# Dilated attention over shared keys in 24 rounds of one group and two heads

## What is computed

```python
def dilated_group(q, k, v, slopes, window, dilation):    # one of three (window, dilation)
    ...
    scores = einsum(q, k) / sqrt(64)                     # 16 heads of 64
    bias = -slopes * distance
    scores = where(valid, scores + bias, NEG_INF)        # causal, within the window, on the dilation's grid
    m = max(scores); p = exp(scores - m); denom = sum(p)
    return p / denom @ v, m + log(denom)

def dilated_attention(x, k, v, w_q, w_o):
    q = (x @ w_q).reshape(bsz, s, 3, 16, 64)             # one set of queries for each group
    outs, lses = [dilated_group(q[:, :, g], k, v, ...) for g in range(3)]
    out = sum(softmax(lses) * outs)
    return out.reshape(bsz, s, 1024) @ w_o
```

## Times and profile before

| what | us |
| --- | --- |
| median of 3 runs | 1826.42 |
| lowest and highest | 1825.64, 1828.47 |
| the profiled execution | 1825.73 |
| its span, first to last instruction | 1824.0 |
| TensorE, VectorE, ScalarE busy in the span | 1772.3, 1290.3, 977.8 |

### The profile page before, as it was taken

The page is one execution under the profiler, slowest core; times in us unless marked ns, Lnnn a source line. Parts: engine busy times, 40 slices in busy tenths (PEclk is TensorE's granted clock), DMA queues, the critical chain, the costliest instruction groups (busy, mean ns, idle before and its releaser), DMA issues.

```text
span 1824.0 us, 33247 instructions
## 1 busy us (share of the span) xinstructions
PE 1772.3 (97%) x11768; PEld 1607.0 (88%) x11768; DVE 1290.3 (71%) x2099; ACT 977.8 (54%) x1706; POOL 0.2 (0%) x4
## 2 busy tenths in 40 slices
PE   8999998999999999999899998999999999999998
PEld 7888998888899888888788888878999988798887
DVE  6776789777655776678877766758656576677765
ACT  5563694655355564555565635454534354556553
POOL 0000000000000000000000000000000000000000
PEclk9999999999999999999999999999999999989999
DMA  7665465466545665323446652333556533346662
GB/s 223 188 205 188 123 197 166 152 189 214 172 143 180 185 201 190 116 93 105 173 153 187 208 182 86 111 104 117 162 172 202 168 98 126 98 131 186 190 206 87
DMA packets 76637, 290.77 MB, mean 159 GB/s; under 512 B 9344, under 2 KB 11648, under 8 KB 76544
## 3 DMA queue, kind: packets, MB, share of 16 engines
q1 hardware_dynamic: 76544, 289.50, 50.2%
HBM read 288.42 MB, written 1.05 MB: 159 GB/s over the span
## 4 chain that ended last, share of the span: by engine, by line
PE 88%; DVE 7%; ACT 3%; issue 1%; DMA 0%; SPq 0%; ACTq 0%; DVEq 0%
PE psum L500 32%; PE psum L501 16%; PE psum L492 11%; PE psum L494 10%; PE psum L493 10%; DVE wlo L1505 2%; PE psum L738 1%; PE psum L632 1%; PE psum L627 1%; DVE r L1677 1%; PE psum L579 1%; PE psum L737 1%; ACT whi L1043 1%; PE psum L860 1%; PE psum L867 1%
## 5 line engine op out<-in xcount | busy, mean ns | idle before, releaser
L1505 DVE TENSOR_TENSOR wlo<-raw,whi 128x1024 fp32r<-128x1024 f32 (+3 forms) x496 | 644.8, 1309 | 262.3 <-ACT whi L1043 261.5
L500 PE MATMUL psum<-x_split,whi 128*128 128x512 f32 x1760 | 618.7, 395 | 4.5 <-DVE x_split L1540 3.4
L1043 ACT ACTIVATE whi<-raw 128x1024 fp32r<-128x1024 f32 (+3 forms) x496 | 548.8, 1119 | 43.0 <-PE psum L494 24.4
L501 PE MATMUL psum<-x_split,wlo 128*128 128x256 f32 x1760 | 494.2, 281 | 0.0
L500 PEld LDWEIGHTS psum<-x_split,whi 128*128 128x128 f32 x1760 | 331.3, 188 | 82.9 <-DVE x_split L1540 2.7
L492 PE MATMUL psum<-x_split,whi 128*128 128x272 f32 (+1 forms) x1184 | 349.4, 295 | 9.8 <-DVE wlo L1505 4.9
L494 PE MATMUL psum<-x_split,wlo 128*128 128x272 f32 (+1 forms) x1184 | 341.4, 288 | 0.0
L493 PE MATMUL psum<-x_split,whi 128*128 128x272 f32 (+1 forms) x1184 | 340.6, 288 | 0.0
L501 PEld LDWEIGHTS psum<-x_split,wlo 128*128 128x128 f32 x1760 | 331.7, 188 | 0.0
L500 PE MATMUL psum<-h_split,whi 128*128 128x512 f32 x770 | 272.2, 397 | 0.0
L492 PEld LDWEIGHTS psum<-x_split,whi 128*128 128x128 f32 x1184 | 226.3, 191 | 20.9 <-issue 14.7
(11 more groups left out here) (230 smaller groups left out, 1767.1 us busy)
## 6 DMA issues: line engine op xcount, KB each, us to landing
raw<-w_in SPq DMA_DIRECT2D x264, 512.0 KB, 3.6
raw<-w_out SPq DMA_DIRECT2D x96, 704.0 KB, 4.3
raw<-w_mix SPq DMA_DIRECT2D x44, 512.0 KB, 3.6
raw<-w_rg SPq DMA_DIRECT2D x25, 512.0 KB, 4.1
raw<-w_q SPq DMA_DIRECT2D x24, 512.0 KB, 3.8
raw<-w_mixo SPq DMA_DIRECT2D x16, 576.0 KB, 3.7
raw<-w_kv SPq DMA_DIRECT2D x16, 512.0 KB, 3.6
raw<-w_rg_out SPq DMA_DIRECT2D x8, 640.0 KB, 3.9
```

Source lines behind the costliest of these rows:

```text
L500: nc.tensor.matmul(ps[:, bank, :], whi[slot][:, w], split, start=start, stop=False)
L501: return nc.tensor.matmul(part(bank, 0), wlo[slot][:, w], split[:, 0], start=False, stop=stop)
L1043: nc.scalar.activation(whi[slot][:, 0:cols], raw[slot][:, 0:cols], ACT.Copy).then_inc(w_hi_done, count)
L1505: V.tensor_tensor(wlo[slot][:, 0:cols], raw[slot][:, 0:cols], f(whi[slot][:, 0:cols]), ALU.subtract).then_inc(w_lo_done, 1)
```

## The change

The attention stage runs in rounds, one behind each projection tile. Round n takes pair n // 3 and group n % 3, and both heads of the pair.

- `scores(n)`: four matmuls, the two heads alternating, head e to bank 2 + 2 (n % 2) + e; it waits for its own projection tile and for VectorE's reading of round n - 2 (`round_biased`).
- `bias_max(n)`: four fused instructions (scores plus distance, times minus the slope, and the minimum), for each head and token tile, and at the third group a small minimum over groups. The slope's reciprocal is folded into the scale of the queries (`C_QS`, eight more columns of parameters). `exps` takes the negative.
- `sum_groups(a)`: one addition and two fused instructions (addition and scaling) in place of two additions and two scalings.
- `values(hp)`: both heads of a pair, alternating, in one bank (7); transposes go to bank 6.
- Two buffers of scores for a pair each: `s_even`, and `s_odd` in rows of `h_split` that are free in this stage.
- After the last tile six steps follow, in which the output projection is begun on three tiles: seven products deep on the first two and five on the third.
- The semaphore counts of the hybrid layers no longer include the attention's sixteen heads.

Of the three loops over s in the diff, the first is TensorE's, the second ScalarE's and the third VectorE's.

```diff
-            def scores(a):
-                hp, rows = a // 2, slice(HD * (a % 2), HD * (a % 2 + 1))
-                pe.wait_ge(acc_free, st.u0 + GROUPS * (hp + 1))
-                if a:
-                    pe.wait_ge(biased, a)
-                for g in range(GROUPS):
-                    nc.tensor.matmul(ps[:, 2 + g, 0:P], qT[rows, hp % 2, g, 0:P], kT[rows, hp, 0:P], start=True, stop=True)
-                    last = nc.tensor.matmul(ps[:, 2 + g, P:SCORES], qT[rows, hp % 2, g, P:SEQ], kT[rows, hp, :],
-                                            start=True, stop=True)
-                last.then_inc(scored, 1)
+            def scores(n):
+                hp, g = n // GROUPS, n % GROUPS
+                pe.wait_ge(acc_free, st.u0 + n + 1)
+                if n >= 2:
+                    pe.wait_ge(round_biased, n - 1)
+                for queries, keys in ((slice(0, P), slice(0, P)), (slice(P, SEQ), slice(0, SEQ))):
+                    for e in range(2):
+                        rows = slice(HD * e, HD * (e + 1))
+                        cols = TOKEN_TILES[queries.start // P]
+                        last = nc.tensor.matmul(ps[:, round_bank(n, e), cols], qT[rows, hp % 2, g, queries], kT[rows, hp, keys],
+                                                start=True, stop=True)
+                last.then_inc(round_scored, 1)
...
+            def values(hp):
+                pe.wait_ge(pT_copied, 2 * hp + 2)
+                if hp:
+                    pe.wait_ge(at_ready, hp)
+                for t in range(2):
+                    for e in range(2):
+                        a = 2 * hp + e
+                        ins = nc.tensor.matmul(ps[HD * e:HD * (e + 1), 7, P * t:SEQ], v_tok[:, t, HD * a:HD * (a + 1)],
+                                               pT[:, e, SEQ * t:SEQ * t + SEQ - P * t], start=t == 0, stop=t == 1,
+                                               skip_group_check=True)
+                        if t:
+                            ins.then_inc(pv_done, 1)
...
+            for s in range(Q_TILES + 6):
+                if s < Q_TILES:
+                    query(s)
+                if s == Q_TILES:
+                    begin_output(0, range(0, 3))
+                if s == Q_TILES + 1:
+                    begin_output(0, range(3, 6))
+                if s == Q_TILES + 2:
+                    begin_output(1, range(0, 3))
+                if s == Q_TILES + 3:
+                    begin_output(1, range(3, 6))
+                if s == Q_TILES + 4:
+                    for j in range(2):
+                        begin_output(j, range(6, 7))
+                if s == Q_TILES + 5:
+                    begin_output(2, range(0, 5))
+                if 1 <= s <= Q_TILES:
+                    scores(s - 1)
+                if s >= 6 and s % 3 == 0:
+                    transposed(2 * (s // 3 - 2))
+                if s >= 6 and s % 3 == 1:
+                    transposed(2 * (s // 3 - 2) + 1)
+                if s >= 6 and s % 3 == 2:
+                    values(s // 3 - 2)
...
+            for s in range(Q_TILES + 7):
+                if s < Q_TILES:
+                    round_ahead(st, s // SLOTS, s % SLOTS)
+                if s >= 8 and s % 3 == 2:
+                    copy_transposed(2 * ((s - 8) // 3) + 1)
+                if s >= 9 and s % 3 == 0:
+                    round_output((s - 9) // 3)
+                if s >= 7 and s % 3 == 1:
+                    copy_transposed(2 * ((s - 7) // 3))
+                if 5 <= s < Q_TILES + 4 and s % 3 == 2:
+                    exps(2 * ((s - 5) // 3))
+                if 6 <= s < Q_TILES + 4 and s % 3 == 0:
+                    exps(2 * ((s - 6) // 3) + 1)
+                if s in (Q_TILES + 3, Q_TILES + 5):
+                    next_chunk(by_name["o"], 0, (s - Q_TILES) // 2 - 1)
+                if s < Q_TILES:
+                    query_tile(s)
...
+            def bias_max(n):
+                hp, g = n // GROUPS, n % GROUPS
+                b = hp % 2
+                dve.wait_ge(round_scored, n + 1)
+                if hp >= 2:
+                    dve.wait_ge(pT_done, 2 * hp - 2)
+                for e in range(2):
+                    for t, cols in enumerate(TOKEN_TILES):
+                        ins = V.tensor_tensor_reduce(s_pair[b][:, e, g, cols], ps[:, round_bank(n, e), cols], dist[:, g, cols],
+                                                     -head_slope(2 * hp + e), 3e38, ALU.add, ALU.min, nmax_g[:, b, e, t, g:g + 1])
+                ins.then_inc(round_biased, 1)
+                if g == GROUPS - 1:
+                    dve.wait_ge(round_biased, n + 1)
+                    V.tensor_reduce(nmax[:, b, :, :], nmax_g[:, b, :, :, :], AX.X, ALU.min).then_inc(nmax_done, 1)
...
+                link(V.tensor_tensor(s[:, e, 1, :], s[:, e, 1, :], s[:, e, 2, :], ALU.add))
+                for t, cols in enumerate(TOKEN_TILES):
+                    ins = V.tensor_tensor_reduce(s[:, e, 0, cols], s[:, e, 0, cols], s[:, e, 1, cols], rden[:, b, e, t:t + 1], 0.0,
+                                                 ALU.add, ALU.add, total[:, b, e, t:t + 1])
...
+            for s in range(Q_TILES + 7):
+                if s < Q_TILES:
+                    rest(s)
+                if 2 <= s < Q_TILES + 2:
+                    bias_max(s - 2)
+                if 5 <= s < Q_TILES + 4 and s % 3 == 2:
+                    sum_groups(2 * ((s - 5) // 3))
+                if 6 <= s < Q_TILES + 4 and s % 3 == 0:
+                    sum_groups(2 * ((s - 6) // 3) + 1)
+                if s >= 9 and s % 3 == 0:
+                    rest_of_output((s - 9) // 3)
+                if s in (Q_TILES + 3, Q_TILES + 5):
+                    rest_of_chunk(*ahead(by_name["o"], 0, (s - Q_TILES) // 2 - 1))
```

More of the change, by code:

```diff
@@ L194, in build @@
     dist = place("dist", [GROUPS, SCORES])
-    s_at = place("s_at", [2, GROUPS, SCORES])
-    nmax = place("nmax", [2, 2])
-    den = place("den", [2, 2])
-    rden = place("rden", [2, 2])
+    s_even = place("s_even", [2, GROUPS, SCORES])
+    nmax_g = place("nmax_g", [2, 2, 2, GROUPS])
+    nmax = place("nmax", [2, 2, 2])
+    den = place("den", [2, 2, 2])
+    rden = place("rden", [2, 2, 2])
+    total = place("total", [2, 2, 2])
     pT = place("pT", [2, SCORES])
+    cursor[0] = hhi_at + KD * TOK * 4
+    s_odd = place("s_odd", [2, GROUPS, SCORES])
+    assert cursor[0] <= hlo_at
+    s_pair = (s_even, s_odd)
     cursor[0] = mix_at
@@ L319, in build @@
     v_copied = sem("v_copied")
+    round_scored = sem("round_scored")
+    round_biased = sem("round_biased")
     scored = sem("scored")
@@ L549, in from_h @@
             first = isinstance(i, int) and i == 0
-            todo = [k for k in range(tiles) if not (begun and first and j < 2 and k in begun)]
+            todo = [k for k in range(tiles) if not (begun and first and k in begun[j])]
             if len(todo) == tiles:
@@ L701, in ready @@
                         pe.wait_ge(rg_ready, n + 1)
-            steps(pe, so.chunks, lambda i, j: from_h(so, i, j, KR, ready=ready, begun=early))
+            steps(pe, so.chunks, lambda i, j: from_h(so, i, j, KR, ready=ready, begun=(early, early, (), ())))
         def keys_values():
@@ L764, in attention @@
-            so, early = by_name["o"], range(PAIRS - 2)
-            for hp in range(PAIRS + 2):
-                a, b, behind = 2 * hp - 2, 2 * hp - 1, 2 * hp - 3
-                if 1 <= hp <= PAIRS:
-                    scores(a)
-                if hp < PAIRS:
-                    query(3 * hp)
-                if hp == PAIRS:
-                    pe.wait_ge(at_ready, PAIRS - 2)
-                    for k in early:
-                        begin(so, 0, k)
-                if 1 <= hp <= PAIRS:
-                    scores(b)
-                if hp >= 2:
-                    transposed(behind)
-                if hp < PAIRS:
-                    query(3 * hp + 1)
-                if hp == PAIRS:
-                    for k in early[:3]:
-                        begin(so, 1, k)
-                if hp >= 2:
-                    values(behind)
-                if 1 <= hp <= PAIRS:
-                    transposed(a)
-                if hp < PAIRS:
-                    query(3 * hp + 2)
-                if hp == PAIRS:
-                    for k in early[3:]:
-                        begin(so, 1, k)
-                if 1 <= hp <= PAIRS:
-                    values(a)
@@ L797, in attention @@
-            steps(pe, so.chunks, lambda i, j: from_h(so, i, j, KD, ready=lambda k: pe.wait_ge(at_ready, k + 1), begun=early))
+            def values(hp):
[10 more added lines that the diff above has]
+                            ins.then_inc(pv_done, 1)
@@ new lines, in attention, with begin_output @@
+            so = by_name["o"]
+            begun = (range(PAIRS - 1), range(PAIRS - 1), range(PAIRS - 3), ())
+            def begin_output(j, tiles):
+                pe.wait_ge(at_ready, tiles[-1] + 1)
+                for k in tiles:
+                    begin(so, j, k)
```

(19 more changed lines are left out.)

125 lines of the change are left out of this document (33 added, 92 removed).

## The result

The changed kernel takes 1808.12 us in the median of four runs (1807.28 to 1810.18), the kernel before 1826.03 beside it (1824.74 to 1828.47): a ratio of 0.9900, 95% interval 0.9888 to 0.9912, so 16.1 to 20.5 us less. A later set of four runs gave 1808.23 (1803.73 to 1809.20), ratio 0.9886 (0.9868 to 0.9904). The prediction of 1806.5 and its range of 1803 to 1813 held. What has to be explained is why the gain is 17.9 us and not 19.9, and whether the reasons given for it are the true ones.

The account below looks back on a forecast made before the run. TensorE, 88% of the chain of waits, bounds the kernel; 19.2 us by the attention stage's end plus 0.7 in the output projection make 19.9, from 1825.73 to 1805.8, median 0.7 above: 1806.5 us; range 1803 to 1813, about 8 in 10.

Parts of the forecast that it names:

- A round: Attention scores on TensorE: one group for two heads at once takes 0.85 us, at most 1.0.
- both heads' values: Attention values on TensorE: two heads in column halves of one bank take 0.79 us, at most 0.96; before 1.58.
- a pair: Steady state of the attention stage: one head pair takes 12.97 us of TensorE, 2.56 less than 15.53.
- step 24: Attention stage, where the tail begins after six triples of steps: predicted to start at 856.0 us.
- the hybrid block: Hybrid layers' twelve two-head matmuls, 1.34 us, 0.35 over pure column time; gave the upper bound of 1.0 for scores.
- (a): Rival, attention steady state: VectorE and ScalarE in lockstep, 14.6 us a pair, total 1818; chance 0.12.
- (b): Rival, attention scores: the two heads don't run at once, 1.5 us for both, total 1827; chance 0.04.
- (c): Rival, VectorE in attention: fused minimum is the bound, slower if over 0.61 us on average, total 1838; chance 0.02.
- (d): Rival, better: the tail's idle stretches are shorter or the clock holds where it fell, 1802 or less; chance 0.08.
- The last rest of output 19.2 earlier: End of the attention tail: last rest of output at 872.1 us in place of 891.27.
- The output projection: Behind the attention stage: VectorE stays the bound, laps of 2.72 us stay, first two tiles gain 0.7 us at full clock.
- which gains nothing: Output projection: 57 products fewer than 192 remain for TensorE, before 36 fewer, with no gain in time.

Follow-up runs that it names:

- e5_apart: Changed kernel with the second head's score matmuls moved behind each step's transposes or values, in 19 of 24 rounds; 1826.21 us.
- e3_unfused: Changed kernel with the fused add-and-minimum split into one 384-column add and two minima for each head; 1809.86 us.
- e4_pad_large: Changed kernel with five extra chained 384-column memsets on VectorE behind each round; 1844.04 us.
- e7: Changed kernel with five extra matmuls ahead of the norm, behind the output projection's last product; 1811.83 us.
- e10: Changed kernel with 20 extra matmuls ahead of the norm, behind the output projection's last product; 1805.67 us.
- e9: Changed kernel with 11, 4, 13 and 6 extra matmuls filling the tail's waiting stretches; 1808.64 us.
- e11_all: Changed kernel with last values ahead of the third tile's products, 11, 4 and 13 extra tail matmuls and 20 ahead of the norm; 1804.92 us.
- e8: Changed kernel with the third output tile's 15 products taken from ahead of the last pair's values, six following behind them; 1805.80 us.

## Why the prediction was right, and where a size was off

**The steady state, right in every term.** A round 0.856 (predicted 0.85, bounds 0.85 to 1.0), both heads' values 0.801 (0.79), a pair 13.00 (12.97). TensorE resumed at 760.27 and began step 24 at 854.54: 94.27 us for a predicted 94.2. Where a bound had to be taken between the attention's own rows and the hybrid block, the row of the same shape was the right one: e5_apart shows 0.85 for one head, 0.65 + 0.20, and the second head adds less than 0.01 to that.

**The other engines, right.** VectorE 10.1 us a pair, under the 11.4 that were counted without the overlap of neighbours; ScalarE 33.91 / 4 = 8.5 for a predicted 8.4. One remark in the prediction fails: that VectorE would have become the bound without the fused minimum. Its own 12.5 us a pair were under 12.97, and e3_unfused has 12.8 in a period of 13.0. The fused minimum gave room and no time in the steady state.

**The rivals.** (a) is refuted by e3_unfused, which has 27% more work on VectorE and the same period. (b) is refuted by the round of 0.856, and e5_apart, with 19 of 24 rounds in series, shows what it costs: 1826, where (b) had 1827. That the two agree is partly chance: a round in series costs 1.81 in e5 and not the 1.5 of (b), but the values of two heads still run at once there. (c) falls by its price: the 16 fused instructions cost 0.37 on average, (12 x 0.352 + 4 x 0.416) / 16, 0.416 being those of the sums, not over 0.61. e4_pad_large shows that the mechanism would be as described once VectorE has more than TensorE. (d), the clock holding in the tail, is what e7 and e10 showed in their profiles without a filled tail; it didn't bring 1802, and no run says what decides it.

**The tail: mechanism right, the clock's term missing.** "The last rest of output 19.2 earlier" was the step that was mis-sized. From the stage's start to the last rest of output there are 872.09 - 752.14 = 119.95 us, before 891.27 - 753.81 = 137.46: 17.5 less. Of the 1.7 that are missing 1.45 is the tail, 17.55 for 16.1. At full clock it takes 16.15 or 16.16 in e7, e9 and e10, so the waits were counted rightly; what the sum left out is the stretch at half clock, which the range had with up to 1.7. A tail at full clock would not have brought all of it to the total, as the norms of e7 and e9 show.

**The output projection: right bound, half the gain.** It stayed VectorE-bound and went from 20.66 to 20.27 us: 0.4 for a predicted 0.7.

**The norm: not in the sum.** It went from 3.94 to 5.48 us, 1.54 more. TensorE came to the output projection with more products done, so it had less left (16.8 us busy for 19.4) while VectorE had the same 18.6; the idle stretch ahead of the norm grew from 1.30 to 3.05, and half clock followed. The prediction saw the 21 products fewer and wrote "which gains nothing"; it costs. e10_warm_norm_full and e11_all show it as cause: with 20 matmuls of no use in that gap the norm takes 3.93 and 3.72, against 5.1 to 6.6 in the eleven executions without them.

The account of the stretch is then 17.5 + 0.4 - 1.5 = 16.4 for a predicted 19.9, and the medians' 17.9 hold about 1.5 us of executions that differ elsewhere. The stretch missed its forecast by 3.5 us and the median by 1.6, so the total came out nearer to the forecast than its parts did, and that is luck.

## What to carry to other kernels

Where two small matmuls can sit in two halves of the array, it's enough to issue them as neighbours; one other shape between them cost the whole gain here. To see what a second engine's list does to the period, add up its work: as long as it stays under TensorE's, even by 2%, it cost nothing here, where its work is ordered a step behind. And when TensorE is given less to do in a stretch that another engine bounds, look at the first matmuls behind it: the longer idle time can be paid back there at half clock.

## What was not expected of the hardware

- Of matmuls of two halves of the rows, issued head by head, the second head's first ones started ahead of the first head's last ones: 0.863 us for the round where tile by tile gave 0.856.
- A block of one head (0.85 us) is as long as one of two heads (0.86).
- Idle stretches in the tail (4.15 us in all in the changed kernel) were followed by half clock in seven profiled executions and by full clock in two. Which it will be was not settled.
- A gap of 1.99 us ahead of the norm (e8) was followed by half clock; after 1.30 (before the change) and 0.67 (e10) the norm ran at full clock.
